# Decode with attention: value pages in four bursts of four pages per sample, where two bursts of eight stood

## The reference, cut to what matters

```python
def gather_pages(pool, layer, page_table):
    g = pool[layer, page_table]
    return g.reshape((g.shape[0], g.shape[1] * g.shape[2]) + g.shape[3:])

# in fox_attention, per block of queries
s = jnp.einsum('bqhd,bkhd->bhqk', q_blk, k).astype(jnp.float32) * scale
s = s + c_q[..., :, None] - c_k[..., None, :]
s = jnp.where(key_pos[None, :] <= q_pos[:, None], s, -jnp.inf)
p = jax.nn.softmax(s, axis=-1).astype(v.dtype)
return jnp.einsum('bhqk,bkhd->bqhd', p, v)
```

## Time and profile before

| | us |
|---|---|
| median of 3 runs | 2663.24 (2662.0 to 2663.32) |
| the profiled execution's own time | 2660.18 |
| its span, first to last instruction | 2658.5 |
| TensorE busy | 2572.5 (97%) |
| VectorE busy | 1241.5 (47%) |
| ScalarE busy | 873.6 (33%) |
| GpSimd busy | 410.6 (15%) |
| DMA, mean over the span | 99 GB/s |
| the decode rounds b = 1 to 7 | 628 to 832, 204 |

### The profile page before, as it was taken

How to read it: one execution, slowest core, us unless ns; L and a number is a source line. 1 busy time by engine, 2 the same in 40 slices (tenths; PEclk the granted TensorE clock), 3 DMA queues, 4 the chain that set the end, 5 groups by cost and what they waited for, 6 DMA issues and landing times.

```text
span 2658.5 us, 51458 instructions
## 1 busy us (share of the span) xinstructions
PE 2572.5 (97%) x20485; PEld 2438.9 (92%) x20485; DVE 1241.5 (47%) x2018; ACT 873.6 (33%) x1542; POOL 410.6 (15%) x602
## 2 busy tenths in 40 slices
PE   8999999998998999999999999999989989999998
PEld 7999999995556999999999999989979969999998
DVE  5444325545554544442444442378646565444423
ACT  4222224214443422232332232244354444222322
POOL 0000003023332200000200000065335542000001
PEclk9999999998999999999999999999999999999999
DMA  4232322247885233233222233223210133332331
GB/s 127 88 88 87 101 81 67 78 130 257 288 294 186 63 91 90 87 100 88 59 87 88 87 103 89 67 64 87 74 36 1 33 98 95 94 88 87 100 88 45
DMA packets 397765, 263.17 MB, mean 99 GB/s; under 512 B 10984, under 2 KB 370613, under 8 KB 397608
## 3 DMA queue, kind: packets, MB, share of 16 engines
q1 hardware_dynamic: 386096, 223.03, 28.9%
q0 software_dynamic: 11536, 38.28, 4.3%
HBM read 251.71 MB, written 9.56 MB: 98 GB/s over the span
## 4 chain that ended last, share of the span: by engine, by line
PE 69%; DVE 4%; ACT 2%; issue 1%; POOL 1%; ACTq 0%; POOLq 0%; DVEq 0%
PE ps L495 50%; PE ps L481 4%; PE ps L2388 2%; PE ps L1445 1%; PE ps L2404 1%; PE ps L1499 1%; PE ps L1458 1%; PE ps L1469 1%; POOL xT L1026 1%; PE ps L538 1%; PE ps L2412 1%; PE ps L509 1%; PE ps L1392 0%; PE ps L2372 0%; PE ps L1414 0%
## 5 line engine op out<-in xcount | busy, mean ns | idle before, releaser
L473 DVE TENSOR_TENSOR w_lo<-w_raw,w_hi 128x1024 fp32r<-128x1024 f32 (+1 forms) x314 | 422.4, 1345 | 970.5 <-ACT w_hi L466 968.8
L495 PE MATMUL ps<-hd_hi,w_hi 128*128 128x272 f32 x3712 | 771.1, 289 | 4.4 <-DVE w_lo L473 4.3
L495 PE MATMUL ps<-hd_lo,w_hi 128*128 128x272 f32 x3712 | 767.4, 288 | 0.0
L495 PE MATMUL ps<-hd_hi,w_lo 128*128 128x272 f32 x3712 | 763.5, 287 | 0.0
L466 ACT CAST w_hi<-w_raw 128x1024 fp32r<-128x1024 f32 (+1 forms) x314 | 351.0, 1118 | 1122.6 <-PE ps L495 1068.0
L495 PEld LDWEIGHTS ps<-hd_hi,w_hi 128*128 128x128 f32 x3712 | 581.1, 188 | 7.8 <-issue 7.4
L495 PEld LDWEIGHTS ps<-hd_lo,w_hi 128*128 128x128 f32 x3712 | 584.4, 189 | 0.0
L495 PEld LDWEIGHTS ps<-hd_hi,w_lo 128*128 128x128 f32 x3712 | 581.8, 188 | 0.0
L1026 POOL TENSOR_TENSOR xT<-xT,rstd_rows 128x272 f32<-128x272 f32 x96 | 84.5, 910 | 1709.7 <-DVE rstd_rows L1051 1709.6
L495 PE MATMUL ps<-h_hi,w_hi 128*128 128x272 f32 x1232 | 255.2, 289 | 0.0
L495 PE MATMUL ps<-h_lo,w_hi 128*128 128x272 f32 x1232 | 254.7, 288 | 0.0
(11 more groups left out here) (529 smaller groups left out, 2985.1 us busy)
## 6 DMA issues: line engine op xcount, KB each, us to landing
w_raw<-in_ffn_w_gate_dram SPq DMA_DIRECT2D x88, 512.0 KB, 3.7
w_raw<-in_ffn_w_up_dram SPq DMA_DIRECT2D x88, 512.0 KB, 3.7
w_raw<-in_ffn_w_down_dram SPq DMA_DIRECT2D x64, 704.0 KB, 4.6
v_pages<-in_cache_a_v_dram POOLq DMA_DIRECT2D x128, 256.0 KB, 4.4
w_raw<-in_c_w_in_dram SPq DMA_DIRECT2D x33, 512.0 KB, 4.0
k_pages<-in_cache_a_k_dram SPq DMA_DIRECT2D x64, 256.0 KB, 4.3
k_pages_raw<-in_cache_a_k_dram SPq DMA_DIRECT2D x64, 256.0 KB, 3.9
w_raw<-in_ab_w_in_dram SPq DMA_DIRECT2D x25, 512.0 KB, 3.9
```

The source lines that it names most:

```text
L473: e.tensor_tensor(w_lo[:, n % 2, 0:nk * P], raw[:, n % RAW, 0:nk * P], w_hi[:, n % 2, 0:nk * P].bitcast(F32), ALU.subtract).then_inc(sem(" ...
L495: mm = e.matmul(ps[:, bank + h, 0:TH], w, x[:, k0 + k, half(h)], start=first and k == 0 and w is wh and x is x_hi, stop=last and k == nk - ...
```

## The change

In rounds b = 1 to 7, the sixteen value pages of sample b - 1 are multiplied in four bursts of four pages instead of two of eight. Pages 4 to 7 now stand behind page turns 9 and 10, ahead of pv. Pages 8 to 11 stay where they were, and between them and pages 12 to 15 now stands page turn 13, which was behind new_values.

```diff
                 new_scores(b)
                 group_turn(b, 0)
-                value_pages(b - 1, range(8))
+                value_pages(b - 1, range(4))
                 turn(4 * b + 1, 4 * b + 2)
                 page_turn(b, 9)
                 page_turn(b, 10)
+                value_pages(b - 1, range(4, 8))
                 e.wait_ge(sem("new_out"), b + 1)
                 pv(2 * b)
                 scores(2 * b + 1)
...
                 group_turn(b, 1)
-                value_pages(b - 1, range(8, PAGES))
+                value_pages(b - 1, range(8, 12))
+                page_turn(b, 13)
+                value_pages(b - 1, range(12, PAGES))
                 e.wait_ge(sem("o_taken"), 2 * b + 1)
                 new_values(b - 1)
-                page_turn(b, 13)
                 turn(4 * b + 2, 4 * b + 3)
```

## The result

The changed kernel takes 2669.92 us (median of 10 runs) against 2662.32 for the kernel before (10 runs): 7.6 us more, ratio 1.0029 with a 95% interval of 1.0019 to 1.0038. It is slower, as forecast (2669.5 us, +6.2). The whole interval shows it slower; its low end, 5.1 us, lies just under the 5.3 us that the prediction took as its bound. The profiled execution of the changed kernel has a span of 2669.5 us against 2658.5, 11.0 more; where these 11.0 us lie is told further down.

The account below looks back on a forecast made before the run. It took TensorE to bound the decode part of the attention layer, busy 184.82 of 204 us. 0.15 + 0.74 = 0.89 us a sample, times seven 6.2, on the median 2663.24 gives 2669.5 us; range 2664.3 to 2674.5.

Parts of the forecast that it names:

- Part A: Pages 4 to 7 behind page turns 9 and 10: two bursts of four 2.00 us against 1.85, +0.15 a sample.
- the way out of the 128-column shape: From page turns 9 and 10 to pv's 64 columns: taken as paid before, 0 more; 0.09 us kept for the range.
- Part B: Page turn 13 between the second burst's halves: 2.59 us instead of 1.85 until L1503, +0.74 us a sample.
- Page turn 15 waits for VectorE's chain: L1508 to page turn 15 stays 2.01 us, set by VectorE's chain; the wait grows from 0.30 to about 0.8 us.
- The wait before the group scores stays: At 648.45, TensorE's 0.73 us wait stays, since VectorE's copy of page 11 is delayed as much as pv.
- queues have nothing to add in the sum: Key page data and value page buffers come in time in the decode rounds, so loads add nothing to 0.89 us a sample.
- Switches: On TensorE, changing tiling mode drains the engine: 0.15 us for a split burst, 0.13 for the moved turn's two ends.
- 1, switches free: TensorE loads next weights while matmuls stream; only uncovered transposes cost, 0.46 us times 7, +3.2 us, 2666.4; chance 8%.
- 2, page turn 13 covered: VectorE's chain does not hold page turn 15, so only tile switches are paid: +3.0 us, 2666.2; chance 6%.
- 3, heads of bursts that cost 0.4 us each: Two more bursts or page turns a sample start with semaphore waits, 0.4 us each: +11.8 us, 2675.0; chance 10%.
- 5, the wait ended by page 10's copy: ScalarE's copy of page 10 ends the 0.73 us wait before the group scores; waits go, -4.2 us, 2659.0; chance 4%.
- 4, the clock: Lower-clock stretches behind the decode stage, about 1.5 us each; two falling away gives +3.2 us, 2666.4; chance 8%.

Follow-up runs that it names:

- copy experiment: Changed kernel with VectorE's copy of page 13 ahead of the output rows: rounds -0.65 us against the kernel before, ratio 0.9995.
- split without a switch: Kernel before, with pages 8 to 11 right behind the group scores, ahead of the group turn, pages 12 to 15 behind it: rounds +0.01 us, ratio 0.9999.
- first split alone: Kernel before, with only pages 4 to 7 moved behind page turns 9 and 10, the second burst left whole: rounds +1.02 us, ratio 0.9999.

## Why the prediction was right, point by point

**Part A, +0.15 us a round:** 0.14 in every round, in the changed kernel and alone. No more for the way out of the 128-column shape, as assumed. pv found nothing to wait for, so the burst filled nothing.

**Part B, +0.74:** 0.73 in every round. Its split into 0.15 + 0.13 for switches and 0.46 for the turn measured 0.30 and 0.43.

**Page turn 15 waits for VectorE's chain:** 2.01 us as before, the wait 0.30 to 0.74 in odd rounds and 0.52 to 0.96 in even ones, forecast 0.8. The copy experiment shows the cause.

**The wait before the group scores stays:** 2.9 us in four rounds, before and after. That it was VectorE's copy of page 11 that ended it, and not ScalarE's of page 10, the timeline of ScalarE shows: the copy of page 10 begins at 644.01 and takes 0.58 us, so it is over 3.9 us ahead of the scores (648.45), and the copy that the row names, at 647.76, is that of page 12, which these scores don't need. In the changed kernel page 10 is turned 0.87 us earlier in its round (8.28 us behind the first L1489, where 9.15 were), and the wait did not move by a hundredth.

**The step that failed**, though the time came out near, is "queues have nothing to add in the sum". It looked at whether data and free buffers come in time, which they do, and not at when GpSimd works. GpSimd kept its distance from the first burst while VectorE came later, and at the start of four rounds its 0.72 us operation met VectorE's small copies or the scaling: +1.8 us. So the sum for the rounds was 6.2 and measured 7.9; 28.80 us between the first two L1508 instead of the 28.5 forecast is round 2's share of it. That the forecast of 2669.5 us lies only 0.4 from the measured 2669.92 is luck: the change was 1.4 us larger than forecast, and the kernel before was 0.9 us faster in the ten runs than in the three.

**Switches:** on the side of the weight loads the engine stands idle for 0.84 us ahead of page turn 13 in the changed kernel (651.45), until the 32-column products are over, and for 0.27 us in the split without a switch, where the burst follows the group scores in their shape. This and the 0.14 us agree with the Trainium skill's rule that a change of tiling mode drains the engine ("TensorEngine Tiling (Array Packing)", Key Properties). That weight loads run ahead on the way out of the 32-column shape, no row shows.

**The rivals.** 1, switches free: no, 0.30 us for the added pair in part B. 2, page turn 13 covered: no, moving it alone costs 0.43 a round. 3, heads of bursts that cost 0.4 us each: no, a split without a switch costs 0.01 us in seven rounds. 5, the wait ended by page 10's copy: no. 4, the clock: it does move a profiled execution. By the starts of matmuls of the same number, the changed kernel lags by 7.9 us at 912 us; at 1785 by 9.1 and at 1982 by 10.8, in a part of the program that the change doesn't touch. There the granted clock is lower than before, 0.86 against 0.93 in 1760 to 1784 and 0.91 against 1.00 in 1950 to 1970:

```profile
1760.00:1784.00 24.00, 19.64 (x137) 19.45 (x137) 15.37 (x19) 7.12 (x20) 10.97 (x30) 0.86 0.26 68
...
1950.00:1970.00 20.00, 16.86 (x120) 11.95 (x119) 9.57 (x43) 11.57 (x33) 6.67 (x7) 0.91 0.37 93
```

That is the greater part of the gap between the 11.0 us of the two spans and the 7.6 of the medians. The first split alone shows the same two values, 0.86 and 0.91, with +1.02 us of rounds, so these falls do not follow the size of the delay. They also differ between executions of one kernel: of the ten of the changed kernel the three shortest (2666.7 to 2668.4 us) have a mean granted clock of 0.992, the longest (2674.2) 0.988. What decides them stays open.

## What to carry to other kernels

A wait of TensorE is filled by work that stands ahead of it, and here that work cost no switch, for it had the tile shape of a neighbour. With VectorE's copy of page 13 early in both, four bursts of four pages gave -0.7 us of rounds where they broke up 128-column work and -10.3 where two of them stood in the waits of the 32-column scores. A filler of another shape was not tried. Before a step is moved forward, look at who must take its result: an early page turn was worth nothing until its copy was moved ahead of what stood before it on VectorE. And when one engine is delayed and another isn't, lay their timelines side by side again, for they may now meet.

## What was not expected of the hardware

Two VectorE copies of 64x16 values (0.17 us each) took 0.89 us beside a GpSimd operation of 0.72 us, and a scaling of 32x32 took 0.85 instead of 0.23; with GpSimd's operation moved away, no copy took more than 0.22 us. In some of these meetings the VectorE operation waited although its record begins first. Four products of one shape follow another four at 0.86 us and the next shape at 1.00, so a change of tile shape cost TensorE about 0.14 us here. A fall of the clock in the rounds cost 1.1 us; it came in two of the eleven kernels that differ from the one before, in different rounds, and each time with a meeting of VectorE and GpSimd nearby that is easily counted with it.
